# Paged attention of a one-core decoder layer: scores and queries handed on ahead of the selection, exponentials a sequence later, rows copied by ScalarE, new values and picks in strips

## The reference

```python
k_past = cache_k[page_table]                      # 8 sequences x 1024 x 8 heads x 128
gate = einsum('bqhd,bnhd->bhqn', q, k_mean)       # mean key of each block of 256
sel = top_k(gate, 3)                              # 3 of the 4 past blocks, and the own one
s = einsum('bqhd,bhqnjd->bhqnj', q, k_g) * d ** -0.5
p = softmax(where(allowed, s, NEG_INF))
o = einsum('bhqnj,bhqnjd->bqhd', p, v_g)          # then @ w_proj_b, gate, merge
```

## Time and profile before

| | before |
|---|---|
| median of 3 runs | 2440.32 us (2436.37 to 2441.68) |
| profiled execution's own time | 2434.05 us |
| its span | 2432.2 us |
| mean granted TensorE clock | 0.973 |
| TensorE busy | 2309.8 us, 95% |
| VectorE busy | 1150.6 us, 47% |
| ScalarE busy | 955.8 us, 39% |
| DMA | 461.17 MB, mean 190 GB/s |

### The profile page before, as it was taken

One profiled execution on the slowest core, in us unless ns is written; L12 is line 12 of the kernel. 1 busy time (PEld: TensorE's weight loads), 2 busy tenths in 40 slices (PEclk: granted clock), 3 DMA queues, 4 the chain that ended last, 5 costly groups with the idle time before them and its releaser, 6 DMA issues. The chain is left out here.

```text
span 2432.2 us, 49500 instructions
## 1 busy us (share of the span) xinstructions
PE 2309.8 (95%) x19762; PEld 2037.3 (84%) x19762; DVE 1150.6 (47%) x1908; ACT 955.8 (39%) x1413; POOL 107.6 (4%) x224
## 2 busy tenths in 40 slices
PE   6999899999999999978998999799999999999998
PEld 3789787878878887645666999799999999999998
DVE  3456635344353543434444555645455555544433
ACT  1433333334343343325433333355454554433333
POOL 0000011010000000100000000000000010000000
PEclk8999999999999999959998999899999999999999
DMA  9885556655666656666997555355555555555544
GB/s 316 276 304 150 150 182 183 187 170 180 185 190 187 183 172 189 209 206 228 342 327 249 157 156 165 100 165 165 165 166 166 166 164 164 164 166 164 164 145 119
DMA packets 326693, 461.17 MB, mean 190 GB/s; under 512 B 37338, under 2 KB 220396, under 8 KB 326076
## 3 DMA queue, kind: packets, MB, share of 16 engines
q1 hardware_dynamic: 318893, 450.39, 59.1%
q10 hardware_dynamic: 7634, 8.38, 1.0%
HBM read 442.83 MB, written 15.86 MB: 189 GB/s over the span
## 5 line engine op out<-in xcount | busy, mean ns | idle before, releaser
L948 ACT ACTIVATE whi<-raw 128x1024 fp32r<-128x1024 f32 (+1 forms) x512 | 526.3, 1028 | 912.3 <-PE ps L1948 882.5
L1948 PE MATMUL ps<-hhi,whi 128*128 128x288 f32 x2736 | 832.6, 304 | 12.1 <-DVE hlo L1447 6.4
L1948 PE MATMUL ps<-hhi,wlo 128*128 128x288 f32 x2736 | 808.4, 295 | 0.0
L1948 PE MATMUL ps<-hlo,whi 128*128 128x288 f32 x2736 | 807.6, 295 | 0.0
L1396 DVE TENSOR_TENSOR wlo<-raw,whi 128x1024 fp32r<-128x1024 f32 (+1 forms) x400 | 470.4, 1177 | 624.6 <-ACT whi L948 624.6
L1948 PEld LDWEIGHTS ps<-hhi,whi 128*128 128x128 f32 x2736 | 515.3, 188 | 76.2 <-issue 55.8
L1948 PEld LDWEIGHTS ps<-hlo,whi 128*128 128x128 f32 x2736 | 515.8, 189 | 1.2
L1948 PEld LDWEIGHTS ps<-hhi,wlo 128*128 128x128 f32 x2736 | 515.2, 188 | 0.0
L1948 PE MATMUL ps<-fhi,whi 128*128 128x288 f32 x704 | 208.0, 295 | 2.8 <-DVE wlo L1396 2.8
L1948 PE MATMUL ps<-fhi,wlo 128*128 128x288 f32 x704 | 207.7, 295 | 0.0
L1948 PE MATMUL ps<-flo,whi 128*128 128x288 f32 x704 | 207.3, 294 | 0.0
(11 more groups left out here) (389 smaller groups left out, 2801.0 us busy)
## 6 DMA issues: line engine op xcount, KB each, us to landing
raw<-in_w_up SPq DMA_DIRECT2D x352, 256.0 KB, 2.9
raw<-in_w_ada SPq DMA_DIRECT2D x128, 512.0 KB, 4.9
raw<-in_w_in SPq DMA_DIRECT2D x112, 512.0 KB, 4.6
raw<-in_w_down SPq DMA_DIRECT2D x88, 512.0 KB, 3.9
kpage<-in_cache_v SPq DMA_DIRECT2D x64, 512.0 KB, 5.1
raw<-in_w_in SPq DMA_DIRECT2D x72, 384.0 KB, 5.4
kpage<-in_cache_k SPq DMA_DIRECT2D x40, 512.0 KB, 5.1
ada_d<-in_w_ada SPq DMA_DIRECT2D x32, 512.0 KB, 4.9
```

Of the source, the lines that this page charges most:

```text
L948: return act.activation(o, i, ACT.Copy, **k)
L1948: return pe.matmul(out, lhsT, rhs, start=start, stop=stop, **k)
```

## The change

The attention's order and shapes are changed, the merge's start too. Nothing else is.

- Constants: `pick4` (32 columns) gives way to `shift4` (88 columns) and `seqrow4` (8 columns). A tile `osum` of 128 x 256 is added, in place of memory that `newconv` uses later.
- VectorE: reading the scores out of PSUM is a function of its own, `new_scores(b)`, which raises `scores_read`; the queries of the next sequence are laid after it and ahead of `select(b)`. `head_scores(b+1)` goes ahead of `normalise(b)`. The half copy of the output row is gone. `out_cols(b)` becomes `out_rows(b)`: the picked rows are multiplied with a column of `seqrow4` and added to `osum`, 256 columns. A new `out_cols()` copies all outputs once, after two transposes.
- ScalarE: `exps(b-1)` goes behind the second key copy of keys(b). `outs(b)` copies the whole row of 1,024. Three slabs of the merge are rounded ahead of the outputs' high half.
- TensorE: the second turn waits for `scores_read` and the queries, not for the selection. `pick_rows` multiplies 32 weight columns of `shift4` with 128 columns of the output row, head by head in four strips. The new values are four products of 256 columns in four strips instead of two of 512 in one. The last pick and the two transposes (`turn_outs`) go behind the first and the second slab of the merge.

```diff
@@ act keys(b)
+                    if p == 1 and b:
+                        exps(b - 1)
                     if p == 2:
                         head_exp(b)
...
             def outs(b):
                 act.wait_ge(seq_done, b + 1)
-                copy(osb[:, 0:CH], pbank(6)).then_inc(seq_rows, 1)
+                copy(osb[:, :], ps[:, 6:8, :].rearrange("p a t -> p (a t)")).then_inc(seq_rows, 1)
 
             keys(0)
             for b in range(NB - 1):
-                exps(b)
                 keys(b + 1)
                 outs(b)
             exps(NB - 1)
             outs(NB - 1)
 
-            for s in range(2):
+            for s in range(3):
                 hi("merge", G(0, None, 0), s)
-            act.wait_ge(seq_copied, 8)
+            act.wait_ge(seq_copied, NB + 1)
             copy(ohi[:, :, :], of[:, :, :]).then_inc(branch_hi, 1)
@@ dve
+            def new_scores(b):
+
+                dve.wait_ge(seq_scored, b + 1)
+                own.inc(dve.tensor_copy(srow2[:, PAST:], pbank(3)[:, 0:m]))
+                TS_(srow2[:, 0:PAST], ps[:, 4:6, :].rearrange("p a t -> p (a t)"), SCALE, None, ALU.mult).then_inc(scores_read, 1)
+
             def select(b):
 
                 row, sg = srow2, smg
-                dve.wait_ge(seq_scored, b + 1)
-                own.inc(dve.tensor_copy(row[:, PAST:], pbank(3)[:, 0:m]))
-                own(TS_(row[:, 0:PAST], ps[:, 4:6, :].rearrange("p a t -> p (a t)"), SCALE, None, ALU.mult))
+                own.wait()
+                dve.wait_ge(scores_read, LAST_COLS + b + 1)
...
-            def outs(b):
-
-                dve.wait_ge(seq_done, b + 1)
-                dve.tensor_copy(osb[:, CH:], pbank(7)).then_inc(seq_rows, 1)
-
-            def out_cols(b):
+            def out_rows(b):
                 dve.wait_ge(seq_out_turned, b + 1)
-                col = slice(TP + TS * b, TP + TS * b + TS)
-                dve.tensor_copy(of[:, :, col], pbank(3)[:, P:P + HB * TS].rearrange("p (h t) -> p h t", t=TS)).then_inc(seq_copied, 1)
+                mine = c("seqrow4")[:, b:b + 1]
+                src = pbank(3 if b < NB - 1 else 7)[:, P:3 * P].rearrange("p (i f) -> p i f", i=2)
+                if b == 0:
+                    TS_(osum[:, :, :], src, mine, None, ALU.mult).then_inc(seq_copied, 1)
+                    return
+                dve.wait_ge(seq_copied, b)
+                STT(osum[:, :, :], src, mine, osum[:, :, :], ALU.mult, ALU.add).then_inc(seq_copied, 1)
+
+            def out_cols():
+                dve.wait_ge(seq_out_turned, NB + 1)
+                dve.tensor_copy(of[:, :, TP:T], pbank(6)[:, 0:2 * P].rearrange("p (h x) -> p h x", x=m)).then_inc(seq_copied, 1)
...
             queries(0)
-            head(0)
+            head_scores(0)
+            head_norm(0)
+            head_out(0)
+            new_scores(0)
+            queries(1)
             select(0)
             for b in range(NB - 1):
-                queries(b + 1)
+                head_scores(b + 1)
                 normalise(b)
-                head(b + 1)
+                head_norm(b + 1)
+                head_out(b + 1)
                 prob_cols(b)
                 if b:
-                    out_cols(b - 1)
+                    out_rows(b - 1)
+                new_scores(b + 1)
+                if b < NB - 2:
+                    queries(b + 2)
                 select(b + 1)
-                outs(b)
             normalise(NB - 1)
             prob_cols(NB - 1)
-            out_cols(NB - 2)
-            outs(NB - 1)
-            out_cols(NB - 1)
-            for s in range(2):
-                lo("merge", G(0, None, 0), s)
+            out_rows(NB - 2)
+            lo("merge", G(0, None, 0), 0)
+            lo("merge", G(0, None, 0), 1)
+            out_rows(NB - 1)
+            lo("merge", G(0, None, 0), 2)
+            out_cols()
             dve.wait_ge(branch_hi, KA + 1)
             TTn(olo[:, :, :], of[:, :, :], ohi[:, :, :].bitcast(F32), ALU.subtract).then_inc(merge_read, 1)
@@ pe
+                    if p == 0 and b > 1:
+                        pe.wait_ge(seq_rows, b - 1)
...
             def pick_rows(b):
 
-                pe.wait_ge(seq_rows, b * 2 + 2)
+                pe.wait_ge(seq_rows, b + 1)
                 for h in range(HB):
-                    own_cols = c("pick4")[:, h * TS:(h + 1) * TS]
-                    i = mm(pbank(3)[:, P + h * TS:P + (h + 1) * TS], osb[:, h * P:(h + 1) * P], own_cols)
-                i.then_inc(seq_out_turned, 1)
+                    i, j = h // 4, h % 4
+                    off = 28 + 8 * j + 4 * i - 4 * b
+                    ins = mm(ps[32 * j:32 * j + 32, 3 if b < NB - 1 else 7, P + i * P:P + (i + 1) * P],
+                             c("shift4")[:, off:off + 32], osb[:, h * P:(h + 1) * P])
+                ins.then_inc(seq_out_turned, 1)
+
+            def turn_outs():
+
+                pe.wait_ge(seq_copied, NB)
+                for i in range(2):
+                    ins = pe.transpose(pbank(6)[:, i * P:(i + 1) * P], osum[:, i, :], ident)
+                ins.then_inc(seq_out_turned, 1)
...
-                for a in range(2):
-                    i = mm(ps[0:m, 6 + a, :], PT2[0:m, NPG, :], vnat[0:m, 2, a * CH:(a + 1) * CH], False, True)
+                for x in range(4):
+                    half = slice(x % 2 * 2 * P, x % 2 * 2 * P + 2 * P)
+                    i = mm(ps[32 * x:32 * x + 32, 6 + x // 2, half], PT2[0:m, NPG, :], vnat[0:m, 2, x * 2 * P:(x + 1) * 2 * P], False, True,
+                           skip_group_check=True)
                 i.then_inc(seq_done, 1)
...
-                    pe.wait_ge(seq_selected, b + 1)
-                    if b:
-                        pe.wait_ge(seq_rows, 2 * b)
+                    pe.wait_ge(scores_read, LAST_COLS + b + 1)
                     pe.wait_ge(query_laid, b + 2)
                 keys(b + 1, b * 64 + 64, rest)
                 values(b, b * 64 + 96)
             values(NB - 1, 32 * 2 * NB)
-            pick_rows(NB - 1)
-
-            pe.wait_ge(seq_copied, 8)
+
+            def last_outs(s):
+                if s == 0:
+                    pick_rows(NB - 1)
+                if s == 1:
+                    turn_outs()
+
+            pe.wait_ge(seq_copied, NB - 1)
             for i in range(4):
                 g = G(0, None, i)
                 if i:
                     pe.wait_ge(merge_read, 2 * i)
-                products("merge", g, 0, 4, 0, yahi, yalo)
+                products("merge", g, 0, 4, 0, yahi, yalo, between=None if i else last_outs)
```

More of the change, by code:

```diff
@@ L103, in shape_constants @@
     add("sum4", (s % 32 == np.arange(NC)[None, :]) * 1.0)
-    x4, col4 = s % 32, np.arange(NB * TS)[None, :]
-    add("pick4", (col4 == (4 * (x4 // TS % 2) + x4 // 8) * TS + x4 % TS) * 1.0)
+    add("shift4", (np.arange(28 + 32 + 28)[None, :] == 28 + s % 32) * 1.0)
+    add("seqrow4", (s % 32 // TS == np.arange(NB)[None, :]) * 1.0)
     add("seq", (s4 // TS == np.arange(NB)[None, :]) * 1.0)
@@ L159, in build @@
         restev = at("restev", [P, 2, T], o)
+        osum = at("osum", [P, 2, P], o)
         ptab = at("ptab", [1, NB * NPG], o + size(2 * T), I32)
@@ L315, in build @@
         HEADS_0 = ADA_X + 48
+        LAST_COLS = 1
         def kfirst_in(p):
@@ L515, in build @@
         root_rows = sem("root_rows")
+        scores_read = last_cols
         stages = {}
@@ L1272, in merge @@
             def merge(g):
-                for s in range(2 if g.first else 0, 8):
+                for s in range(3 if g.first else 0, 8):
                     hi("merge", g, s)
@@ L2532, in values @@
                             strip = slice(32 * (p % 4), 32 * (p % 4) + 32)
-                            i = mm(ps[strip, 6 + a, :], PT2[:, p, :], kpage[:, p, a * CH:(a + 1) * CH], p < 4, p >= 5)
+                            i = mm(ps[strip, 6 + a, :], PT2[:, p, :], kpage[:, p, a * CH:(a + 1) * CH], p < 4, False, skip_group_check=True)
                             if a:
                                 i.then_inc(values_used, 1)
-                for a in range(2):
-                    i = mm(ps[0:m, 6 + a, :], PT2[0:m, NPG, :], vnat[0:m, 2, a * CH:(a + 1) * CH], False, True)
+                for x in range(4):
+                    half = slice(x % 2 * 2 * P, x % 2 * 2 * P + 2 * P)
+                    i = mm(ps[32 * x:32 * x + 32, 6 + x // 2, half], PT2[0:m, NPG, :], vnat[0:m, 2, x * 2 * P:(x + 1) * 2 * P], False, True,
+                           skip_group_check=True)
                 i.then_inc(seq_done, 1)
```

## The result

| | before | after | ratio, 95% interval |
|---|---|---|---|
| first series, median | 2438.76 us (4 runs) | 2412.48 us (4 runs) | 0.9889 (0.9864 to 0.9913) |
| second series, median | 2432.54 us (17 runs) | 2414.92 us (5 runs) | 0.992 (0.9907 to 0.9933) |
| profiled executions, own time | 2434.05 us | 2406.09 and 2414.92 us | |
| mean granted TensorE clock | 0.973 | 0.976 and 0.973 | |

The change is faster by 26 us in the first series. In the second, which has more runs, it is faster by 19.5 us by the ratio (0.8% of 2432.54) and by 17.6 us between the two medians. I had forecast 16, and 2424 us with a range from 2413 to 2433. The traces say how much of it is the change.

A forecast was written before the change was run, and what follows sets the result against it. TensorE, busy 95%, was taken to bound the kernel, with DMA close and becoming the bound after the change. Periods -16.2, start -4.9 and tail +4.8 sum to -16.3 us from 2440.32: 2424 us, range 2413 to 2433.

The forecast's parts named there:

- Periods: Steady sequences of the paged attention: six periods fall from 25.1 to 22.4 us each, -16.2 us in all.
- the rate of the loads: Page loads in steady sequences: taken as 375 GB/s, giving 22.4 us for the 8.39 MB of a sequence.
- TensorE's own period: TensorE's work per steady sequence: savings of 0.85, 1.4 and 1.33 us bring 24.78 us down to 21.2.
- picks and start of the values: Steady sequences on TensorE: values start some 2.15 us after the Snew transpose instead of 3.00, 0.85 us saved.
- new values: Steady sequences on TensorE: products over four overlapping strips take 0.45 us instead of 1.83, 1.4 us saved.
- first scoring: Steady sequences: first scoring starts 2.4 us after the next sequence's first page turn instead of 3.73, 1.33 us saved.
- Stretches at half clock: Steady sequences: 0.3 us of the old 25.1 us period, over the quiet one, counted for half clock.
- Start: First sequences of the paged attention: third scoring -5.3, clock +1.8, new values of sequence 0 -1.4, together -4.9 us.
- the 1.8 us for the clock: Start of the attention: loss to the 1.2 GHz level after the moved wait, 0 to 2.4 us, taken as 1.8.
- Tail: Last sequence and first merge group: -1.65 + 0.85 + 3.3 + 2.3, together +4.8 us.
- the rival in which TensorE stays the bound: Steady sequences: load queue kept full at some 400 GB/s, period 21.2 to 21.5 us, 2418 us; chance 0.16.
- the slower case: Steady sequences: SyncE's load queue empties, rate falls to 323 GB/s, period 26.0 us, 2446 us; chance 0.06.

The follow-up runs named there:

- the strip run: The changed kernel with the new values in one strip again, two products of 512 columns; ratio 0.9931 (0.9903 to 0.9958), period 22.50 us.

## Why the prediction was off

The direction, the mechanism and most terms held; the forecast of 16.3 us was too small by 4 to 5 in the stretch, and 3 of these are the periods. The rest of the distance to the first series' 26 us lies outside the stretch.

- **Periods, -16.2 forecast, -18.9 and -19.5 measured.** The step that failed is the rate of the loads. I scaled 343 GB/s at share 0.94 to 365, and took 375. The changed kernel moves 397 over 25 us and 379 over 120 us (1130 to 1250). A period of 21.9 us asks for 383, and 22.4 us a period became 21.9. The rate of 343 before says what the kernel asked for, 338 GB/s at its period of 24.78, and not what the loads can do: SyncE stood 28.9 of 120 us for a free place, and 10.4 after. The short windows of the earlier trace rows had said so. The Trainium skill's figure of 358 GB/s (DMA: Bandwidth & Descriptors, "Where 436 GB/s comes from") is a memory's rate shared by two cores. Here one core runs, and 397 over 25 us is beyond it, so taken as a cap it would have forecast worse than I did.
- **TensorE's own period, 21.2 forecast, 21.05 measured**, term by term: picks and start of the values 0.96 saved instead of 0.85, new values 1.25 (from the strip run) instead of 1.4, first scoring 1.52 instead of 1.33. Right; the first two misses nearly cancel.
- **Stretches at half clock.** I kept 0.3 us of them in the old period and gave them back; the changed loop has granted clock 1.00 from 1130 to 1250. Right.
- **Start, -4.9 forecast.** Taken as the forecast did, from the first turn to the first turn of `keys(2)`, it is -4.9 and -6.6 (47.2 us before; 42.3 and 40.5 after). The moved wait was 2.39 us in both executions, instead of 3. In the first a stretch at half clock followed it, as the scoring of 1.08 us shows. In the second none did: the scoring takes 0.64 us and the granted clock is 1.00 from 1125 to 1140. So the 1.8 us for the clock is a term that comes or stays away, and the forecast's exact hit in the first execution has luck in it.
- **Tail, +4.8 forecast.** From the new values of sequence 6 to the gating it is +2.5 and +3.7, and 1.2 more when taken from the next start, as the forecast did: +3.8 and +4.9. The merge starts 2.5 and 2.3 us earlier by that mark (1.65 forecast), and its first group takes 6.2 and 7.3 us longer (6.45 forecast). The wait for the fourth slab was 3.23 us where 3.3 stood, with half clock behind it.
- **The rest.** In the profiled pair what remains is the 7.5 us ahead of the stretch. In the medians it is drift between runs and series whose place no trace shows: the kernel before alone moved by 6.2 us. The forecast and the range were built on its median of three runs, 2440.32, and had no term for such a move.

The measured period of 21.9 us lies between the forecast's 22.4 and the 21.2 to 21.5 of the rival in which TensorE stays the bound. Both limits act: 21.05 us are TensorE's own, and the loads add the rest. That strips overlap, and that the loads have no cap at 365, is shown; the slower case is excluded by the interval.

## What to carry to other kernels

When the same engine lays an input for the next stage and does a long decision for this one, hand on the input first, and look at every other queue for the next instruction that waits for the decision: it must be moved behind the work that others need, or it only inherits the wait. A load rate read where the issuing queue waits for free places says nothing about the cap. Ask for that queue's own waits, take the best windows at full share for one end of the range, and expect two limits a few per cent apart to share what either saves. Work moved past a queue's end goes ahead of what stood there: count what the next stage's first buffers wait for.

## What was unexpected of the hardware

- Loading 64 of 128 partitions of a page did not shorten it in proportion: 319 GB/s at share 0.97, and from 1130 to 1250 us these loads of 256 KB landed after a median of 6.3 us where the whole pages in the same trace took 5.5 to 6.3. In the kernel before, whose queue was less full, the same half pages landed after a median of 4.7 us and whole pages after 4.8 to 5.9, so the delay goes with the full queue too. The Trainium skill (DMA: Bandwidth & Descriptors, "Where 436 GB/s comes from") has sixteen ports on the side of SBUF as the ceiling; that half the partitions lie on fewer of them would fit, and no run here shows it.
- Matmuls with only 32 rows, in four column strips, overlap as those with 128 do: eight of 256 columns end after 0.63 us where four of 512 in one strip took 1.90.
- A wait of the same length need not cost the same clock. In the changed kernel's first execution the waits of 2.39 and 3.23 us were followed by a stretch at 1.2 GHz, as the granted clock shows (0.81 from 1120 to 1125, 0.50 from 1305 to 1310). In the second the wait of 2.39 us was not (1.00 from 1125 to 1140), and that goes with the 1.2 us between the 25.1 and 23.9 of the table. The page waits of the loop, 1.0 us at most, were not followed by it either (1.00 from 1130 to 1250).
- The start of the stretch differs by 12 us between profiled executions (1096.2 to 1108.3) while the 1091 us behind its end repeat within 2.4, whichever kernel it is. Compare stretches between like events, not only whole times.
